# Weight-block sums by accumulating DMAs, and two plain pairs ahead of the first seven-product chunk

## The chip, the core and the metric

One NeuronCore of a Trainium2 chip. The metric is the device time of one execution in microseconds, the median of the runs. The engines are named PE (matmuls), VectorE (DVE), ScalarE (ACT), GpSimd (POOL) and SyncE (SP).

## The reference, cut to what matters

Four transformer-like layers over 640 tokens (512 of a sample, 128 of a prompt) with 1024 features, in float32. Layer kinds are conv, pool, attention, conv; each layer ends in a gated feed-forward stage:

```python
hs = modulate(rms_norm(xs, norm2_w[i]), mod_s[3], mod_s[4])
xs = xs + mod_s[5] * swiglu(hs, ffn_in_w[i], ffn_out_w[i])   # the same for xp
# swiglu: hidden = silu(h @ gate_w) * (h @ up_w);  out = hidden @ out_w
# ffn_in_w: (1024, 2 * 2816), ffn_out_w: (2816, 1024)
```

The 2816 hidden features are 22 tiles of 128. A tile needs one tile of gate columns and one of up columns: a pair. The change touches the feed-forward input product of the last layer only.

## The kernel before

**Precision and the plain way.** Each float32 product is made of three float32r matmuls: high part by high part, high by low, low by high. ScalarE makes the high part of weights (a copy into w_hi), VectorE the low part (raw minus w_hi, into w_lo). In the plain way, of layers 0 to 2, weights go in units of 128 columns by 1024 rows, four to a quad, two pairs to a quad. `h_unit` runs 8 x 3 x 2 = 48 matmuls a unit (L700, 320 columns, and L701), so 96 a pair.

**Seven products.** In the last layer (`FIRST_SEVEN = [3, 3, 3, 0]`) all 22 pairs, in chunks of 8, 8 and 6, are made by a seven-product scheme of Strassen's kind (Winograd's form). Tokens are cut into two halves of 320 (and two columns for the shift), features into two halves of 512, gate and up are the two column halves. `product` (L754) runs 4 x 3 = 12 matmuls of 322 columns, and a pair has 7 products, 84 matmuls. For this the kernel needs sums of activations, t1 to t4 (four rows each), and sums of weight blocks, s1 to s4:

- s1 = up rows 0-511 + up rows 512-1023, in `tmp[:, 2]` (product 5; for the very first pair tmp[:, 3])
- s3 = gate first half - up first half, in place of up's first half (product 7)
- s2 = s1 - gate first half, in place of gate's first half (product 6)
- s4 = gate second half - s2, in place of gate's second half (product 3)

Products 1, 2 and 4 use blocks as loaded. GpSimd makes the sums with four 128 x 512 instructions a pair, in `s13` and `s24`: L592 (s1), L596 (s3), L603 (s2), L607 (s4). Each waits on `block_lo_ready` for the split of the block that it overwrites.

**Order.** `ORDER` gives the blocks: for p >= 1, (p,1), (p-1,4), (p,5), (p,6), (p,2), (p,7), (p,3). w_hi and w_lo hold four blocks; block b goes where block b-4 was, once that product is done. ScalarE (`block_hi`, L1252) and VectorE (`block_lo`, L1817) work strictly in their written order between the copy-outs: on ScalarE after (p,7) comes the split of (p+1,5), after (p,3) that of (p+1,6), then the copy-out of product (p+1,1) (L1299) and the split of (p+1,2). The split of (p,3) stands ahead of the copy-outs L1306 and L1310, on the second of which PE's product (p,7) waits. SyncE reloads the raw slots of a pair (two 512 KB loads) when block (p,4) is split. L1923 on VectorE adds product 7 to the up half; PE's product (p,4) waits for it.

**The start of the stage.** GpSimd makes t1 to t4 out of h as its rows become ready (L554 to L569), VectorE the last row (L1861 to L1866); ScalarE and VectorE split them (`turn_step`: t1 after the first unit of the last output quad, a row of t2 to t4 after each other, the last in the seven-product chunk). PE begins the stage with product (0,1) while rows of h still come.

Of the kernel before, what the change touches and what calls it, by code (L numbers as in the profile page):

```python
# [26 lines left out]
KD = D // P  # L27
# [81 lines left out]
SEVEN = 7  # L109
T_STEPS = 4 * HALF  # L110
# [26 lines left out]
ORDER = {n: _order(n) for n in (CHUNK, LAST)}  # L137
# [4 lines left out]
LAYER_S = [sum(max(FT - CHUNK * FIRST_SEVEN[n], 0) for n in range(i)) for i in range(DEPTH + 1)]  # L142
# [3 lines left out]
def _pairs_before(layer, c):  # L146
    return LAYER_S[layer] + CHUNK * (c - FIRST_SEVEN[layer])
# [19 lines left out]
def build(nc, d):  # L167
    with ExitStack() as ctx:
# [99 lines left out]
        s_made = sem("s_made")  # L268
# [118 lines left out]
        def s1_home(p, norm):  # L387

            return tmp[:, 3 if norm and p == 0 else 2, 0:HW]

        def block_source(p, m, norm):

            j = 2 * (p % 2)
            return {1: raw[:, j, 0:HW], 6: raw[:, j, 0:HW], 2: raw[:, j, HW:2 * HW], 3: raw[:, j, HW:2 * HW],
                    7: raw[:, j + 1, 0:HW], 4: raw[:, j + 1, HW:2 * HW], 5: s1_home(p, norm)}[m]
# [11 lines left out]
        def bank_y(p, norm):  # L407

            return ps[:, 2, 0:TW] if norm and p == 0 else ps_sum[:, 1, 0:TW]
# [119 lines left out]
        def _(pool):  # L529
# [45 lines left out]
            def s13(layer, c, p, q, n, norm):  # L575

                first, j, qq = _pairs_before(layer, c), 2 * (p % 2), q + p // 2
                gate_w, up_w = raw[:, j, :], raw[:, j + 1, :]
                pool.wait_ge(raw_in[j], 16 * qq + 16)
                pool.wait_ge(raw_in[j + 1], 16 * qq + 16)  # L580
                if norm and p == 0:
                    if KIND[layer] == "attn":
                        pool.wait_ge(head_ready, HEAD_ROWS)
                elif norm and p == 1:
# [24 lines left out]
            def begin_chunk(layer, c, q, n, norm, turns):  # L609

                s13(layer, c, 0, q, n, norm)
                if turns:
                    t234_of(layer, 2)
                s24(layer, c, 0, n, norm)

            def rest_of_chunk(layer, c, q, n, norm, triples):

                for p in range(1, n):
                    if p % 2 == 1 and p > 1 and p // 2 < len(triples):
                        ada_triple(triples[p // 2])  # L620
                    s13(layer, c, p, q, n, norm)
                    s24(layer, c, p, n, norm)
# [8 lines left out]
            for layer in range(DEPTH):  # L631
# [34 lines left out]
                for c in range(FIRST_SEVEN[layer], 3):  # L666
                    tiles, norm = CHUNK if c < 2 else LAST, c == 0
                    qc = q + c * (Q_IN + Q_OUT)
# [13 lines left out]
        def _(pe):  # L682
# [30 lines left out]
            def h_quads(q, n, count, first=True, late=False):  # L713
# [21 lines left out]
                with pe.Fori(1 if first else 0, count) as i:  # L735
                    for j in range(4):
                        h_unit(i + q, j, n)

            def seven_chunk(layer, c, q, n, norm):

                first, place = _pairs_before(layer, c), PLACE[n]
                row, turns = 2 * layer + 1, c == FIRST_SEVEN[layer]

                def product(p, m, out, a_hi, a_lo, begin, row_ready=None):
# [4 lines left out]
                    for k in range(HALF):  # L749
                        if row_ready is not None:  # L750
                            pe.wait_ge(h_ready, row_ready + k + 1)
# [10 lines left out]
                def p1(p):  # L762
# [5 lines left out]
                    if norm and p == 1:  # L768
                        pe.wait_ge(c11_out, first + 1)
                    product(p, 1, bank_x(p), h_hi[:, 0:HALF, 0:TW], h_lo[:, 0:HALF, 0:TW], True, H_BASE[row] if turns and p == 0 else None)  # L770

                def p2(p):

                    if norm and p == 0:
                        pe.wait_ge(freed[1], 2 * q + 1)
                    else:
                        pe.wait_ge(c11_out, first + p)
                    if norm and p == 1:
                        pe.wait_ge(rms_ready, row + 1)
                    product(p, 2, bank_y(p, norm), h_hi[:, HALF:KD, 0:TW], h_lo[:, HALF:KD, 0:TW], True,  # L780
                            H_BASE[row] + HALF if turns and p == 0 else None)
# [21 lines left out]
                def p6(p):  # L803

                    pe.wait_ge(p1_kept, first + p + 1)
                    if p == 0:
                        turned_rows(T_STEPS - 2)
                    product(p, 6, bank_x(p), t2_hi, t2_lo, False)

                def p7(p):  # L810

                    pe.wait_ge(u2_kept, first + p + 1)
                    if p == 0:
                        turned_rows(T_STEPS - 1)
# [5 lines left out]
                if norm:  # L820
                    sum_features(sq_sum, sq_added, (KD - 1) * (row + 1), sum_ready)
# [347 lines left out]
            for layer in range(DEPTH):  # L1169
# [34 lines left out]
        def _(act):  # L1204
# [23 lines left out]
            def ffn_in_quad(q, i, products, tiles=(KD,) * 4, norm=None):  # L1228
                for j in range(4):
                    step(q, j, tiles[j])  # L1230
                    if j == 0 and norm:
# [11 lines left out]
            def block_hi(n, b, first, q, norm):  # L1243
# [6 lines left out]
                else:  # L1250
                    act.wait_ge(s_made, 4 * (first + p) + {5: 1, 7: 2, 6: 3, 3: 4}[m])
                act.activation(block_home(w_hi, n, b), block_source(p, m, norm), ACT.Copy).then_inc(block_hi_ready, 1)  # L1252

            def first_blocks(layer, c, q, j):

                n = CHUNK if c < 2 else LAST
                for b in {2: (0, 1), 3: (2, 3)}[j]:
                    block_hi(n, b, _pairs_before(layer, c), q, c == 0)
# [1358 lines left out]
```

## Time and profile before

| what | value |
|---|---|
| time, median of 3 runs | 2658.68 us (2658.28 to 2659.0) |
| span of the profiled execution | 2656.5 us, instructions 45073 |
| what lies around its span, to the median | 2.2 us |
| granted TensorE clock, mean | 0.994 |
| seven-product stage, first to last L754 | 2194.8 to 2601.6 us |

The profiled execution is one execution; its span goes from the first to the last instruction. A line such as L754 is a line of the kernel. Matmuls overlap, so a busy PE still has a cadence that is to be read from counts.

### The profile page before, as it was taken

How to read it: one execution, taken by the hardware profiler on the slowest of the kernel's cores; microseconds unless marked ns; L12 is line 12 of the kernel's file. 1: busy time of each engine (PE TensorE's matmuls, PEld its weight loads, DVE VectorE, ACT ScalarE, POOL GpSimd, SP SyncE). 2: the span in 40 equal slices, each digit the busy share in tenths (PEclk: the TensorE clock that was granted, in tenths of full speed). 3: DMA queues.
4: the chain of work that ended last, by engine and by line, in shares of the span. 5: the costliest groups of instructions: out<-in, count | busy, mean ns of one | idle time of the engine just before them, and what ended most of it. 6: DMA issues, size and time to landing. Idle time of an engine off the chain costs nothing.

```text
span 2656.5 us, 45073 instructions
## 1 busy us (share of the span) xinstructions
PE 2626.7 (99%) x17374; PEld 2554.8 (96%) x17374; DVE 1869.1 (70%) x3118; ACT 895.5 (34%) x1346; POOL 252.5 (10%) x300
## 2 busy tenths in 40 slices
PE   9999999999999999999999999999999998999998
PEld 5999999999999999999967999999999997999998
DVE  5898778676586776846775678777465559949486
ACT  4223331212342222124675431221232235425253
POOL 0000001000000000000000000000000034324040
PEclk9999999999999999999999999999999998999999
DMA  7444445354224544422102245444222221212222
GB/s 301 150 144 141 127 134 174 126 159 140 75 80 127 158 150 127 151 69 84 40 13 80 89 136 163 135 139 138 59 88 75 71 64 48 97 63 81 95 75 77
DMA packets 85625, 295.19 MB, mean 111 GB/s; under 512 B 10112, under 2 KB 13312, under 8 KB 85248
## 3 DMA queue, kind: packets, MB, share of 16 engines
q1 hardware_dynamic: 60016, 200.74, 23.0%
q0 software_dynamic: 25488, 92.81, 11.2%
q8 instruction: 79, 1.29, 0.2%
q14 instruction: 42, 0.34, 0.0%
HBM read 290.63 MB, written 2.88 MB: 110 GB/s over the span
## 4 chain that ended last, share of the span: by engine, by line
PE 89%; DVE 6%; issue 2%; ACT 1%; POOL 1%; DMA 1%; DVEq 0%; ACTq 0%; SPq 0%; POOLq 0%
PE ps L700 39%; PE ps L701 39%; PE ps L754 4%; DVE w_lo L1817 1%; PE ps_x L1010 1%; PE ps L986 1%; PE ps_sum L754 1%; DVE tmp L1935 1%; PE ps_sum L997 1%; PE ps L1142 1%; DMA mix<-in_ada_head 1%; DVE w_lo L1702 0%; PE ps L1093 0%; ACT w_hi L1207 0%; PE ps L867 0%
## 5 line engine op out<-in xcount | busy, mean ns | idle before, releaser
L1702 DVE TENSOR_TENSOR w_lo<-raw,w_hi 128x1024 fp32r<-128x1024 f32 (+2 forms) x315 | 376.1, 1194 | 459.2 <-ACT w_hi L1207 458.0
L1207 ACT ACTIVATE w_hi<-raw 128x1024 fp32r<-128x1024 f32 (+2 forms) x315 | 325.1, 1032 | 910.9 <-PE ps L701 899.1
L700 PE MATMUL ps<-h_hi,w_hi 128*128 128x320 f32 x1536 | 479.9, 312 | 0.7 <-DVE h_lo L2031 0.7
L701 PE MATMUL ps<-h_lo,w_hi 128*128 128x322 f32 x1536 | 478.5, 312 | 0.0
L700 PE MATMUL ps<-h_lo,w_hi 128*128 128x320 f32 x1536 | 477.4, 311 | 0.0
L701 PE MATMUL ps<-h_hi,w_lo 128*128 128x322 f32 x1536 | 477.4, 311 | 0.0
L700 PE MATMUL ps<-h_hi,w_lo 128*128 128x320 f32 x1536 | 477.1, 311 | 0.0
L701 PE MATMUL ps<-h_hi,w_hi 128*128 128x322 f32 x1536 | 476.1, 310 | 0.0
L1730 DVE CUSTOM_DVE_ANT_0 ps_x<-ada_w,cond 128x1024 f32<-128x1024 f32 x354 | 436.0, 1232 | 33.5 <-DVE tmp L1778 12.9
L701 PEld LDWEIGHTS ps<-h_hi,w_hi 128*128 128x128 f32 x1536 | 291.1, 190 | 0.5
L701 PEld LDWEIGHTS ps<-h_hi,w_lo 128*128 128x128 f32 x1536 | 291.3, 190 | 0.0
L700 PEld LDWEIGHTS ps<-h_hi,w_hi 128*128 128x128 f32 x1536 | 289.6, 189 | 1.3 <-DVE h_lo L2031 0.8
L700 PEld LDWEIGHTS ps<-h_hi,w_lo 128*128 128x128 f32 x1536 | 290.5, 189 | 0.0
L701 PEld LDWEIGHTS ps<-h_lo,w_hi 128*128 128x128 f32 x1536 | 289.6, 189 | 0.0
L700 PEld LDWEIGHTS ps<-h_lo,w_hi 128*128 128x128 f32 x1536 | 288.4, 188 | 0.0
L700 PE MATMUL ps<-g_hi,w_hi 128*128 128x320 f32 x884 | 274.7, 311 | 3.1 <-DVE x L1991 2.6
L701 PE MATMUL ps<-g_hi,w_lo 128*128 128x320 f32 x884 | 273.6, 309 | 0.0
L700 PE MATMUL ps<-g_hi,w_lo 128*128 128x320 f32 x884 | 273.5, 309 | 0.0
L701 PE MATMUL ps<-g_lo,w_hi 128*128 128x320 f32 x884 | 273.4, 309 | 0.0
L701 PE MATMUL ps<-g_hi,w_hi 128*128 128x320 f32 x884 | 273.4, 309 | 0.0
L700 PE MATMUL ps<-g_lo,w_hi 128*128 128x320 f32 x884 | 273.4, 309 | 0.0
L540 POOL DMA_DIRECT2D ada_w<-in_ada_w x177 | 94.0, 531 | 1729.7 <-DVE ada_raw L1730 1351.7
(244 smaller groups left out, 4220.1 us busy)
## 6 DMA issues: line engine op xcount, KB each, us to landing
raw<-in_weights SPq DMA_DIRECT2D x323, 512.0 KB, 3.6
ada_w<-in_ada_w POOLq DMA_DIRECT2D x177, 512.0 KB, 3.8
raw<-in_weights SPq DMA_DIRECT2D x32, 384.0 KB, 3.0
mix<-in_ada_head SPq DMA_DIRECT2D x16, 512.0 KB, 10.4
x<-in_x SPq DMA_DIRECT2D x8, 320.0 KB, 9.8
out_y<-mix SPq DMA_DIRECT2D x16, 160.0 KB, 1.9
mix<-in_spread SPq DMA_DIRECT2D x1, 1088.0 KB, 5.6
cond<-in_cond SPq DMA_DIRECT2D x1, 1024.0 KB, 14.9
```

What stands on the lines that cost most here:

```text
L540: pool.dma_start(ada_w[:, j * D:(j + 1) * D], d["ada_w"][ADA_N * qa + (j - LEAD)]).then_inc(ada_in[j], 16)
L700: pe.matmul(ps[:, 2 * slot, 0:TA], w[:, slot, ws], a(k)[:, 0:TA], start=begin, stop=end)
L701: mm = pe.matmul(ps[:, 2 * slot + 1, 0:width - TA], w[:, slot, ws], a(k)[:, TA:width], start=begin, stop=end)
L754: mm = pe.matmul(out, w[:, ws], a[:, k, :], start=begin and k == 0 and i == 0, stop=k == HALF - 1 and i == 2, skip_group_check=True)
L986: pe.matmul(out[:, 0:TS], row[:, qt * P:(qt + 1) * P], key[:, 0:TS], start=True, stop=True)
L997: mm = pe.transpose(sum_flat[:, k * P:(k + 1) * P], tmp[:, n % 2, k * P:(k + 1) * P], ident[:])
L1010: pe.matmul(ps_rot, val, of_sample[:, k, :], start=(k == 0), stop=(k == 4))
L1142: mm = pe.matmul(head_row[g % 2], cond_k[:, 2 * pair + k, :], head_w[:, n % HEAD_SLOTS, k * HEAD_W * P:(k + 1) * HEAD_W * P], start=(pair ...
L1207: act.activation(w_hi[:, j % 2, 0:tiles * P], raw[:, j, 0:tiles * P] if src is None else src, ACT.Copy).then_inc(w_hi_ready, 1)
L1702: dve.tensor_tensor(w_lo[:, j % 2, 0:tiles * P], raw[:, j, 0:tiles * P] if src is None else src, w_hi[:, j % 2, 0:tiles * P].bitcast(F32), ...
L1730: dve.tensor_tensor_reduce(ada_products, ada_w[:, j * D:(j + 1) * D], cond[:, v, :], 1.0, 0.0, ALU.mult, ALU.add, ada_raw[:, j, v:v + 1]). ...
L1817: dve.tensor_tensor(block_home(w_lo, n, b), block_source(p, m, norm), block_home(w_hi, n, b).bitcast(F32), ALU.subtract).then_inc(block_lo ...
```

## The change

Constants and chunk sizes: the first chunk of the last layer gets two plain pairs (one quad) ahead of 6 seven-product pairs; the chunks are then 6, 8 and 6.

The sums are made by DMAs issued from GpSimd's queue, 256 KB each. An accumulating DMA adds its source to its destination. s1 is a copy of up's first half from the weights in HBM into tmp[:, 2] and an addition of up's second half from HBM; s3 adds gate's first half from HBM to the raw up half; s2 adds s1 (SBUF) to gate's first half; s4 adds the new s2 (SBUF) to gate's second half. All are sums, with no difference: s3 = gate + up, s2 = gate + s1, s4 = second half + s2. The signs go into the activations: t1, t2 and t4 are split with a factor of -1, and the up result takes a factor of -1 when it is scaled by rinv. (The host hands in the up columns as before.) GpSimd waits for the copy of s1 before it issues the addition to it, for s1 before s2, and for s2 before s4.

```diff
+T1_ROWS = [(), (0,), (1, 2), (3,)]
+T2_ROWS = [(), (0, 1), (2,), (3,)]
+PLAIN_PAIRS = 2
+SEVENS = [CHUNK - PLAIN_PAIRS, CHUNK, LAST]
...
+            def s13(layer, c, p, q, n):
                 first, j, qq = _pairs_before(layer, c), 2 * (p % 2), q + p // 2
+                gate_w, up_w = d["weights"][4 * qq + j], d["weights"][4 * qq + j + 1]
+                if p == 0 and c == 0:
                     pool.wait_ge(sum_ready, 2 * layer + 2)
                 elif p:
                     pool.wait_ge(block_lo_ready, SEVEN * first + PLACE[n][p - 1, 5] + 1)
+                    pool.wait_ge(s2_made, 16 * (first + p))
                 elif c > FIRST_SEVEN[layer]:
                     pool.wait_ge(block_lo_ready, SEVEN * first)
-                pool.tensor_tensor(s1_home(p, norm), up_w[:, 0:HW], up_w[:, HW:2 * HW], ALU.add).then_inc(s_made, 1)
+                    pool.wait_ge(s2_made, 16 * first)
+                pool.dma_start(s1_home, up_w[:, 0:HW]).then_inc(s1_begun, 16)
+                pool.wait_ge(raw_in[j + 1], 16 * qq + 16)
+                pool.dma_start(raw[:, j + 1, 0:HW], gate_w[:, 0:HW], accum_op=ALU.add).then_inc(s3_made, 16)
+                pool.wait_ge(s1_begun, 16 * (first + p + 1))
+                pool.dma_start(s1_home, up_w[:, HW:2 * HW], accum_op=ALU.add).then_inc(s1_made, 16)
+            def s2(layer, c, p, n):
                 first, j = _pairs_before(layer, c), 2 * (p % 2)
                 pool.wait_ge(block_lo_ready, SEVEN * first + PLACE[n][p, 1] + 1)
-                pool.wait_ge(s_made, 4 * (first + p) + 1)
-                pool.tensor_tensor(up_w[:, 0:HW], gate_w[:, 0:HW], up_w[:, 0:HW], ALU.subtract).then_inc(s_made, 1)
+                pool.wait_ge(s1_made, 16 * (first + p + 1))
+                pool.dma_start(raw[:, j, 0:HW], s1_home, accum_op=ALU.add).then_inc(s2_made, 16)
+            def s4(layer, c, p, n):
                 pool.wait_ge(block_lo_ready, SEVEN * first + PLACE[n][p, 2] + 1)
-                pool.wait_ge(s_made, 4 * (first + p) + 3)
-                pool.tensor_tensor(gate_w[:, HW:2 * HW], gate_w[:, HW:2 * HW], gate_w[:, 0:HW], ALU.subtract).then_inc(s_made, 1)
+                pool.wait_ge(s2_made, 16 * (first + p + 1))
+                pool.dma_start(raw[:, j, HW:2 * HW], raw[:, j, 0:HW], accum_op=ALU.add).then_inc(s4_made, 16)
...
-                        seven_chunk(layer, c, q, tiles, c == 0)
+                        h_quads(q, 2 * layer + 1, PLAIN_PAIRS // 2, late=kind == "pool")
+                        seven_chunk(layer, c, q + PLAIN_PAIRS // 2, tiles - PLAIN_PAIRS)
...
-                act.activation(t1_hi[:, k, :], t2_full[:, k, :], ACT.Copy).then_inc(t_hi_ready, 1)
+                act.activation(t1_hi[:, k, :], t2_full[:, k, :], ACT.Identity, scale=-1.0).then_inc(t_hi_ready, 1)
...
+                if turns:
+                    act.wait_ge(unit_done, 4 * q)
+                    for k in range(HALF):
+                        t3_hi_of(layer, k)
                 after_p1(0)
                 after_p5(0)
                 only_refill(0, 2)
+                if turns:
+                    for k in range(HALF):
+                        t4_hi_of(layer, k)
...
-                    dve.tensor_tensor(up_row(p)[:, 0:TA], bank_x(p)[:, 0:TA], rinv[:, 0:TA], ALU.mult).then_inc(c21_out, 1)
+                    dve.scalar_tensor_tensor(out=up_row(p)[:, 0:TA], in0=bank_x(p)[:, 0:TA], scalar=-1.0, in1=rinv[:, 0:TA],
+                                             op0=ALU.mult, op1=ALU.mult).then_inc(c21_out, 1)
```

The second part of the diff is PE's order for the first chunk, the third ScalarE's, the last VectorE's. GpSimd's order for pair 0 is s13, t2 to t4 of row 2, s2, the same of row 3, s4; for every later pair s13, s2, s4. The turned rows are split in other places: t1 in the last output quad (`T1_ROWS`: rows after its second, third and fourth unit), t2 in the plain quad (`T2_ROWS`), t3 and t4 in the chunk, t3 once the plain quad's last unit is done. GpSimd makes the last row too, where VectorE did. Gone too are the waits of the first chunk on rows of h and on the sum of squares (`norm`, `row_ready`), since the plain quad stands there now.

## Rows read from the trace of the kernel before

**Rows 1.** The page, busy us of each engine and their share of the span.

```profile
PE 2626.7 (99%) x17374; PEld 2554.8 (96%) x17374; DVE 1869.1 (70%) x3118; ACT 895.5 (34%) x1346; POOL 252.5 (10%) x300
```

**Rows 2.** By stretch: PE, PEld, DVE, ACT, POOL busy (count), PEclk, DMA share, GB/s.

```profile
2176.00:2230.00 54.00, 37.93 (x193) 36.17 (x192) 41.78 (x59) 23.36 (x45) 30.90 (x26) 0.78 0.09 29
2230.00:2242.00 12.00, 12.00 (x83) 12.00 (x82) 11.70 (x18) 6.25 (x13) 4.52 (x4) 1.00 0.25 88
262.00:304.00 42.00, 42.00 (x282) 41.68 (x281) 34.28 (x52) 16.44 (x21) 2.27 (x5) 1.00 0.41 126
1476.00:1530.00 54.00, 54.00 (x364) 53.68 (x363) 38.20 (x58) 23.43 (x29) 1.59 (x3) 1.00 0.32 98
```

**Rows 3.** PE of line L754 alone, by stretch; seven-product chunks 1 and 2.

```profile
2350.00:2480.00 130.00, 100.53 (x672) 1.00 0.23 82
2500.00:2620.00 120.00, 75.15 (x504) 1.00 0.23 75
```

**Rows 4.** Waits of PE, 2155 to 2232 us: total, times, longest.

```profile
PE ps L754 <- issue: 5.5, 1, 5.5
PE ps L754 <- ACT tmp L1299: 4.0, 1, 4.0
PE ps L754 <- DVE x L1991: 3.8, 1, 3.8
PE ps L700 <- DVE x L1991: 2.6, 1, 2.6
```

**Rows 5.** The timeline of GpSimd, one pair of chunk 1.

```profile
2410.17 1.29 POOL L607 TENSOR_TENSOR raw<-raw 128x512 f32<-128x512 f32 x1 [4.75 <-DVE w_lo L1817]
...
2415.25 1.29 POOL L596 TENSOR_TENSOR raw<-raw 128x512 f32<-128x512 f32 x1 [2.10 <-DVE w_lo L1817]
2416.62 1.61 POOL L603 TENSOR_TENSOR raw<-tmp,raw 128x512 f32<-128x512 f32 x1
2422.99 1.29 POOL L607 TENSOR_TENSOR raw<-raw 128x512 f32<-128x512 f32 x1 [4.75 <-DVE w_lo L1817]
```

**Rows 6.** Who waited for VectorE line L1923, whole span: us, times.

```profile
  PEld ps L754: 2.1, 5
```

**Rows 7.** The timeline of ScalarE, the same pair.

```profile
2418.32 0.63 ACT L1252 ACTIVATE w_hi<-raw 128x512 fp32r<-128x512 f32 x1 [1.28 <-POOL raw L603]
2420.04 0.44 ACT L1299 ACTIVATE tmp<-ps 128x320 f32<-128x320 f32 x1 [1.08 <-PE ps L754]
2420.37 0.63 ACT L1252 ACTIVATE w_hi<-raw 128x512 fp32r<-128x512 f32 x1
```

**Rows 8.** The timeline of VectorE, the same pair.

```profile
2419.76 0.68 DVE L1817 TENSOR_TENSOR w_lo<-tmp,w_hi 128x512 fp32r<-128x512 f32 x1
```

**Rows 9.** VectorE groups in a plain stage of layer 2, 1500 to 1600 us.

```profile
L1778 DVE TENSOR_TENSOR tmp<-ps,tmp 128x640 f32<-128x640 f32 x15 | 12.2, 815 | 0.0
...
L1789 DVE SCALAR_TENSOR_TENSOR tmp<-tmp,bias 128x512 f32<-128x512 f32 x7 | 5.3, 752 | 0.9
...
L1789 DVE SCALAR_TENSOR_TENSOR tmp<-tmp,bias 128x128 f32<-128x128 f32 x7 | 2.4, 346 | 0.0
```

**Rows 10.** ScalarE groups, 1500 to 1600 us.

```profile
L1219 ACT ACTIVATE g_hi<-tmp 128x640 f32 x7 | 5.2, 741 | 24.1 <-DVE tmp L1789 24.1
```

**Rows 11.** VectorE line L1941: durations in ns, minimum, median, maximum.

```profile
L1941 DVE TENSOR_TENSOR g_lo<-tmp,g_hi x22: 810/1894/1909, 2234.4 to 2604.7; 128x640 fp32r<-128x640 f32 x22
```

**Rows 12.** The DMA view, issues: count, KB each, median us to landing.

```profile
raw<-in_weights SPq DMA_DIRECT2D x323, 512.0 KB, 3.6
ada_w<-in_ada_w POOLq DMA_DIRECT2D x177, 512.0 KB, 3.8
...
mix<-in_spread SPq DMA_DIRECT2D x1, 1088.0 KB, 5.6
...
raw<-in_weights SPq DMA_DIRECT2D x4, 256.0 KB, 2.5
```

**Rows 13.** GpSimd line L540, issues of 512 KB: ns, minimum, median, maximum.

```profile
L540 POOL DMA_DIRECT2D ada_w<-in_ada_w x177: 530/530/699, 36.0 to 1824.3; - x177
```

More of the change, by code:

```diff
@@ L405, in bank_z @@
             return ps[:, 2 * (p % 2) + 1, 0:TW]
-        def bank_y(p, norm):
-            return ps[:, 2, 0:TW] if norm and p == 0 else ps_sum[:, 1, 0:TW]
+        bank_y = ps_sum[:, 1, 0:TW]
         def gate_row(p):
@@ L734, in h_quads, with seven_chunk, product @@
                         h_unit(q, j, n, first=True)
[L735 to L739, printed above, removed]
+                if count > 1 or not first:
+                    with pe.Fori(1 if first else 0, count) as i:
+                        for j in range(4):
+                            h_unit(i + q, j, n)
+            def seven_chunk(layer, c, q, n):
                 first, place = _pairs_before(layer, c), PLACE[n]
-                row, turns = 2 * layer + 1, c == FIRST_SEVEN[layer]
-                def product(p, m, out, a_hi, a_lo, begin, row_ready=None):
+                turns = c == FIRST_SEVEN[layer]
+                def product(p, m, out, a_hi, a_lo, begin):
                     b = place[p, m]
@@ L767, in p1 @@
                         pe.wait_ge(c21_out, first + p - 1)
-                    if norm and p == 1:
-                        pe.wait_ge(c11_out, first + 1)
-                    product(p, 1, bank_x(p), h_hi[:, 0:HALF, 0:TW], h_lo[:, 0:HALF, 0:TW], True, H_BASE[row] if turns and p == 0 else None)
+                    product(p, 1, bank_x(p), h_hi[:, 0:HALF, 0:TW], h_lo[:, 0:HALF, 0:TW], True)
                 def p2(p):
[L774 to L781, printed above, removed]
+                    pe.wait_ge(c11_out, first + p)
+                    product(p, 2, bank_y, h_hi[:, HALF:KD, 0:TW], h_lo[:, HALF:KD, 0:TW], True)
                 def p3(p):
@@ L1226, in gate, with ffn_in_quad @@
                 a.then_inc(gate_ready, 1)
-            def ffn_in_quad(q, i, products, tiles=(KD,) * 4, norm=None):
+            def ffn_in_quad(q, i, products, tiles=(KD,) * 4, norm=None, first=None, turns=None):
                 for j in range(4):
                     step(q, j, tiles[j])
+                    if first is not None and j >= 2:
+                        first_blocks(*first, j)
                     if j == 0 and norm:
@@ L1241, in ffn_in_quad, with block_hi @@
                         g_hi_of(pair_b[:, j // 2, :], bass.ds(2 * i + j // 2, 1) if not isinstance(i, int) else slice(2 * i + j // 2, 2 * i + j // 2 + 1))
-            def block_hi(n, b, first, q, norm):
+                    if turns is not None:
+                        for k in T2_ROWS[j]:
+                            t2_hi_of(turns, k)
+            def block_hi(n, b, first, q):
                 p, m = ORDER[n][b]
@@ L1271, in t234_hi_of @@
-                act.activation(t4_hi[:, k, :], t4_full[:, k, :], ACT.Copy).then_inc(t_hi_ready, 1)
-            def turn_step(layer, j):
-                if j == 0:
-                    for k in range(HALF):
-                        t1_hi_of(layer, k)
-                else:
-                    t234_hi_of(layer, j - 1)
-            def seven_chunk(layer, c, q, n, r, g, tiles, norm):
-                first, place, row = _pairs_before(layer, c), PLACE[n], 2 * layer + 1
+                act.wait_ge(t_lo_ready, T_STEPS * LAYER_T[layer] + 2 * HALF + k + 1)
@@ L1290, in refill @@
                     for b in REFILL[n][place[p, m]]:
-                        block_hi(n, b, first, q, norm)
+                        block_hi(n, b, first, q)
                 def after_p1(p):
-                    if norm and p < 2:
-                        act.wait_ge(sq_added, (KD - 1) * (row + 1))
-                    else:
-                        act.wait_ge(product_ready, r + p - 1)
+                    act.wait_ge(product_ready, r + p - 1)
                     done(p, 1)
@@ L1791, in times, with ffn_in_quad @@
                 v.then_inc(product_ready, 1)
-            def ffn_in_quad(q, i, count, pairs, products, ada=None, tiles=(KD,) * 4, norm=None):
+            def ffn_in_quad(q, i, count, pairs, products, ada=None, tiles=(KD,) * 4, norm=None, first=None, turns=None):
                 for j in range(4):
+                    if first is not None and j >= 2:
+                        first_blocks(*first, j)
                     step(q, j, tiles[j])
@@ L1948, in seven_chunk @@
                 after_p2(0)
-                if norm:
-                    inverse_rms(row)
+                if turns:
+                    for k in range(HALF):
+                        t4_lo_of(layer, k)
                 after_p6(0)
@@ L2321, in attention @@
                         shift_lo(2 * layer + 1)
-                    out_quad(q + half, 4 * half, 2 * layer + 1, gate_of(GATE1), (KD, KD, 0, 0) if half and seven else (KD,) * 4, True,
-                             first=(layer, 0, q + Q_OUT) if half and seven else None, turns=layer if half and seven else None)
+                    out_quad(q + half, 4 * half, 2 * layer + 1, gate_of(GATE1), (KD,) * 4, True, turns=layer if half and seven else None)
             def tail(q, gate):
```

197 lines of the change are left out of this document (94 added, 103 removed).

## The prediction

> **What bounds the kernel now.** I read the page's busy shares first: PE 99%, VectorE 70%, GpSimd 10% [rows 1]. A core in which PE never rests gains only where matmuls disappear, where PE waits, or where its clock is low. So I looked for stretches in which PE does fewer matmuls than its cadence allows. The view by stretches shows one around the change: from 2176 to 2230 us PE ran 193 matmuls in 54 us at a mean granted clock of 0.78 [rows 2]. At the cadence of the seven-product pairs, 672 matmuls in 100.5 us or 0.150 us each [rows 3], these are worth 29 us: 25 us are lost. The waits of PE say how: four waits of 2.6, 3.8, 5.5 and 4.0 us, 15.9 in all [rows 4]; the rest is half clock (0.78 is 44% of the stretch at 1.2 GHz, its other level being 2.4). The same passage into a plain feed-forward stage, in layers 0 and 2, has PE busy throughout at clock 1.00 [rows 2]. That is the loss the two plain pairs can take away.
>
> Then the seven-product stage. A pair is seven products of 12 matmuls: 100.53/8 = 12.57 us, 1.80 us a product. GpSimd's rows show a period of 12.82 us (2410.17 to 2422.99) [rows 5]: PE is the bound, with short waits for L1923 on VectorE, 2.1 us in five times over the whole stage [rows 6].
>
> **What the change takes away and adds, term by term.**
>
> Two plain pairs: 2 x 96 matmuls at 0.148 us (364 in 54 us [rows 2]) = 28.5 us, against 2 x 12.57 = 25.1: **+3.4**.
>
> The passage: PE now works on the plain quad while t1 and t2 are made. What stays is the end of the quad. After its last unit ScalarE splits two blocks (0.63 us each [rows 7]), VectorE makes their low parts (0.68 each [rows 8]), takes the row out (0.82) and multiplies (0.75 + 0.35) [rows 9], about 4.1 us after that unit with the small steps between; ScalarE then makes g_hi, 0.74 [rows 10], five turned rows and the copy that the product (0,6) waits for, six of about 0.44 [rows 7]: 7.5 us, where PE wants (0,6) after three products, 5.4. A gap of 2.1, one of about 1 at (0,7), 2 more for the half clock that such a gap brings (24 us at half clock beside 15.9 of waits in [rows 2, 4]), 1 in the output quad, where t1 on VectorE is now spread over three units: 6 of the 25 stay. **-19**.
>
> GpSimd's arithmetic: while it reads SBUF, VectorE's 640-column subtraction takes 1.89 us instead of 0.81 (median and minimum of L1941 [rows 11]). The Trainium skill has the rule (SBUF — State Buffer, the part on who interferes with whom: a VectorE instruction with two SBUF inputs contends with a GpSimd instruction that reads SBUF); the trace agrees. VectorE isn't the bound, so it is worth at most the waits for L1923: **-2.1 if nothing else holds the pairs, 0 if something does**. The extra multiplications by -1 lie on VectorE operations that exist already: 0.
>
> The DMAs decide. Each pair now needs five of 256 KB on GpSimd's queue, in code order: s1 copy, s3 add, s1 add, s2 add, s4 add. The old four instructions took 1.3 to 1.7 us each, and GpSimd had 7 us of idle time a pair (4.75 before L607, 2.10 before L596) [rows 5].
>
> - A plain 256 KB load took 2.5 us from SyncE's queue; GpSimd's 512 KB took 3.8 where SyncE's took 3.6 [rows 12]. So the copy: 2.7 us, 0.53 of it issue [rows 13]. From 512 to 1088 KB the time grew by 2.0 us, 0.87 for 256 KB [rows 12].
> - No row shows an accumulating DMA or one that reads SBUF to write SBUF. Below, it costs what a copy does, 2.7. Its destination must be read besides the source, a second 256 KB: 2.7 + 0.87 = 3.6. If the write also comes in turn: 4.4. I take L = 3.6, the size with an extra stream, and keep 2.7 and 4.4 for the range. The Trainium skill (DMA: Bandwidth & Descriptors, anatomy of one DMA) gives 2.0 us + bytes/436 GB/s, an estimate of 2.6 us here, with no other term for an addition; by that the first rival below would hold, at 2641.
>
> Now the loop. Let t0 be the end of the low part of block (p,2); before, the s4 instruction starts there (2410.17, 2422.99) [rows 5]. GpSimd issues s4(p), then the s1 copy of pair p+1, which sits behind it in the queue although it needs only block (p,5) and s2(p). The copy lands at 0.6 + 2.7 + 1.17 = t0+4.5; 1.17 is s4's data, 2 x 0.87, less the 0.6 of head start. s3 lies beside it. The s1 add lands at t0+8.1, the s2 add at t0+11.7. Then ScalarE must split (p+1,6), copy out the first product and split (p+1,2), and VectorE makes the low part: 0.63 + 0.33 + 0.63 + 0.68 and small steps = 2.4 [rows 7, 8]. Period: 14.05 us. Before, L603 ended at t0+8.07 and the next t0 was at 12.82, so 4.75 us were there where 2.4 suffice: slack of 2.3 us, and the DMAs eat 3.6. To this come SyncE's two weight loads a pair, 512 KB each, on the same 16 engines: I add 1.0 (bounds 0 and 1.7, the data time of an addition doubled). **Period 15.05 us, 2.5 more than PE needs.**
>
> How often? Pair 0 of each of the three chunks (6, 8 and 6 pairs) has its sums made during the quad before. Pair 1 is 0.9 us within its time: s2(1) lands at 1.3 + 12.65 = 13.95 after the chunk's start, and (1,6) can wait for it until 9 x 1.8 - 1.4 = 14.8. Pair 2 stalls 1.6, each later one 2.5: 9.1 + 14.1 + 9.1 = **+32.3**. These stalls fall on PE before products (p,6) and (p,7), the latter because ScalarE holds at block (p,3) for s4 (3.6 after t0) with the copy-outs for (p,7) behind it.
>
> Sum: +32.3 + 3.4 - 19 = +16.7 us. On the profiled execution, 2656.5 us, that is 2673; on the median of the runs, which lies 2.2 above, **2675**.
>
> **The rivals.**
>
> *The accumulating DMAs are hidden* (ends on the other side). If an addition costs a copy's 2.7 us, s2 lands at 0.6 + 2.7 + 0.3 + 5.4 = t0+9.0, the period of the loop is 11.4, or 12.4 with 1.0 of loads, and PE stays the bound. Then -19 + 3.4 - 2.1 = -17.7: 2641. For it: GpSimd idle more than half of each pair [rows 5]; DMA share in this stretch only a quarter [rows 2]. Against: the chain is three landings deep, and share says nothing of latency. It decides at 14 x g - 2.7 = 15.6, so a surplus g of 1.3 us a pair, which is L = 3.2 us; my two-stream size is above that, a copy's below.
>
> *Additions much slower than two streams.* L = 4.4, with s3 0.7 in the way of the s1 add and 1.7 of loads: s2 lands at t0+14.8, period 18.9, +85 - 15.6 = +70: 2729. Each further us of L adds 3 us a pair, 42 in all, so L = 5.1 gives 2760. For it: the kind of DMA isn't in the trace at all.
>
> *Half clock on top.* The gaps of 2.6 to 5.5 us brought about 6 us of half clock each [rows 2, 4]. If every stall of 2.5 does this, PE needs 12.6 + 3 = 15.6 a pair instead of 15.05: +8 more, 2683. It would add to the forecast, not change its sign; counted in its range.
>
> *The change doesn't do what it says* (additions in order but the plain quad stalls like the old start): the passage gives back only 10 of 19; with the main loop 2684. Against: layers 0 and 2.
>
> **Numbers.** Tell-apart bound: 0.2%, 5.3 us. Forecast (additions between 3.3 and 4 us) 0.38, giving 2664 to 2695; much slower 0.20; hidden 0.30; between hidden and forecast, near break-even, 0.12, of which 0.08 is within 0.2% and 0.04 below. So faster 0.34, same 0.08, slower 0.58. Range 2638 to 2755: it takes in the hidden case and L up to 5.
>
> **What would show it.** In the new trace: in the 54 us around the passage some 330 matmuls or more instead of 193, at a clock near 1; five GpSimd DMA issues a pair with additions landing at 3.6 us; a period of some 15 us between s4 issues; ScalarE's split waiting for DMA rather than for GpSimd; PE waits for w_lo of (p,6). VectorE's L1941 row falls to 0.81. I am wrong if additions land in under 3.2 us, or if the queue doesn't delay the copy behind s4.

## The result and the profile after

The changed kernel takes 2725.62 us (median of 4 runs, 2720.09 to 2725.99); the kernel before took 2658.53 in the same session (4 runs, 2658.28 to 2659.0). The ratio is 1.0247, interval 1.0233 to 1.0262: 67 us slower. The profiled execution took 2725.99, its span 2724.3. Direction and range were right, the size was not: +67 against a forecast of +17.

The page of the kernel after, busy time of each engine, beside [rows 1]:

```profile
PE 2650.6 (97%) x17398; PEld 2572.0 (94%) x17398; DVE 1800.8 (66%) x3097; ACT 882.3 (32%) x1330; POOL 211.0 (8%) x317
```

PE has the 24 more matmuls that two plain pairs cost, and rests 74 us instead of 30. VectorE and GpSimd are both less busy, and yet the kernel is slower: the busy shares don't show the cause.

By stretch, after (columns as in [rows 2]), and then the third stretch in the kernel before. In the kernel after, the second chunk's pairs run from 2370.8 to 2509.4 us, so the third stretch has 20 us of the output product at its end; the fourth is one long period of those pairs:

```profile
2176.00:2230.00 54.00, 52.56 (x352) 51.86 (x351) 43.34 (x65) 26.27 (x49) 32.32 (x32) 1.00 0.39 91
2230.00:2242.00 12.00, 10.96 (x72) 10.43 (x72) 7.65 (x15) 5.96 (x12) 3.17 (x4) 1.00 0.75 180
2390.00:2530.00 140.00, 120.03 (x704) 116.80 (x704) 72.95 (x134) 48.31 (x93) 25.62 (x32) 0.89 0.55 128
2408.90:2429.30 20.40, 16.95 (x89) 16.48 (x89) 9.52 (x18) 6.57 (x14) 4.10 (x6) 0.80 0.52 117
```

```profile
2390.00:2530.00 140.00, 139.72 (x944) 139.15 (x943) 101.12 (x153) 53.86 (x94) 39.20 (x27) 1.00 0.24 83
```

The first line is the passage from the output product into the stage: 352 matmuls where [rows 2] has 193. The plain quad nearly fills it, as in layers 0 and 2. The third line is the loss: in 140 us PE ran 704 matmuls instead of 944, at a granted clock of 0.89. What PE waited for there (waits of PE, 2190 to 2680 us, in us, times, longest), and what ScalarE waited for:

```profile
PE ps L765 <- DVE w_lo L1829: 38.9, 16, 3.6
PE ps L765 <- ACT tmp L1311: 20.1, 15, 2.6
PE ps L765 <- ACT tmp L1300: 1.4, 1, 1.4
```

```profile
ACT w_hi L1261 <- DMA raw<-tmp: 73.2, 15, 6.5
...
ACT w_hi L1261 <- DMA raw<-raw: 58.7, 19, 3.7
ACT w_hi L1261 <- DMA tmp<-in_weights: 43.4, 15, 7.6
```

PE's 38.9 us for w_lo (nearly all ahead of product (p,6)) and 20.1 us for the copy-out L1311 (ahead of product (p,7)) are the two places that the prediction named. One step back, ScalarE stands before its split for each of the three sums in turn: s2 (`raw<-tmp`) 73.2 us, s4 (`raw<-raw`) 58.7, s1 (`tmp<-in_weights`) 43.4. Nothing waits for s3.

GpSimd's timeline over one pair shows the loop itself. L615 is s4, L595 the s1 copy, L598 s3, L601 the s1 addition, L608 s2; each row is an issue (for a DMA the second number is the time of the issue), and the bracket the idle time before it:

```profile
2464.63 0.85 POOL L615 DMA_DIRECT2D raw<-raw  x1 [7.66 <-DVE w_lo L1829]
2465.17 0.89 POOL L595 DMA_DIRECT2D tmp<-in_weights  x1
2465.72 1.23 POOL L598 DMA_DIRECT2D raw<-in_weights  x1
2469.75 0.86 POOL L601 DMA_DIRECT2D tmp<-in_weights  x1 [2.80 <-DMA tmp<-in_weights]
2474.14 0.86 POOL L608 DMA_DIRECT2D raw<-tmp  x1 [3.54 <-DMA tmp<-in_weights]
2481.87 0.85 POOL L615 DMA_DIRECT2D raw<-raw  x1 [6.87 <-DVE w_lo L1829]
```

From one s4 to the next 17.24 us. Over all 17 such intervals inside the chunks, the means from the starts of the issues are 5.45 from s4 to the s1 addition, 4.56 on to s2 and 7.79 on to the next s4: a period of 17.81 (16.0 to 20.3). PE needs 12.57 for a pair: 5.24 too many, 17 times, is 89 us. The DMA view gives the landings, all issued by GpSimd:

```profile
tmp<-in_weights POOLq DMA_DIRECT2D x40, 256.0 KB, 4.3
...
raw<-in_weights POOLq DMA_DIRECT2D x20, 256.0 KB, 5.1
raw<-tmp POOLq DMA_DIRECT2D x20, 256.0 KB, 5.2
raw<-raw POOLq DMA_DIRECT2D x20, 256.0 KB, 3.3
```

The first row mixes the s1 copy (median 4.4) with the s1 addition (3.8, by source line). s4 lands in 3.3. s2 is mostly issued just after SyncE's weight loads of 512 KB (in the pair above 2.2 us after two of them) and has a median of 5.2. In the four cases in which the last load was over 6 us old it landed in 3.2 to 3.3; with a load at most 2.6 us old it took 4.9 to 6.8, but for one of 3.8.

VectorE's subtraction, which took 1894 ns in the median [rows 11], is relieved as forecast, and nothing comes of it:

```profile
L1935 DVE TENSOR_TENSOR g_lo<-tmp,g_hi x20: 815/819/826, 2240.4 to 2672.3; 128x640 fp32r<-128x640 f32 x20
```

### The profile page after: what moved, and what is told of

It reads as the page before. It is cut to its first block and busy times, and to the rows that moved or that the text cites. A ratio compares the mean times of both kernels' runs of the same rounds, so it can differ in the third digit from the quotient of the medians.

```text
span 2724.3 us, 45071 instructions
## 1 busy us (share of the span) xinstructions
PE 2650.6 (97%) x17398; PEld 2572.0 (94%) x17398; DVE 1800.8 (66%) x3097; ACT 882.3 (32%) x1330; POOL 211.0 (8%) x317
## 3 DMA queue, kind: packets, MB, share of 16 engines
q8 instruction: 79, 1.29, 0.2%
## 5 line engine op out<-in xcount | busy, mean ns | idle before, releaser
L712 PE MATMUL ps<-h_hi,w_hi 128*128 128x320 f32 x1568 | 490.0, 313 | 0.7 <-DVE h_lo L2027 0.7
L713 PE MATMUL ps<-h_lo,w_hi 128*128 128x322 f32 x1568 | 488.5, 312 | 0.0
L712 PE MATMUL ps<-h_lo,w_hi 128*128 128x320 f32 x1568 | 487.3, 311 | 0.0
L713 PE MATMUL ps<-h_hi,w_lo 128*128 128x322 f32 x1568 | 487.3, 311 | 0.0
L712 PE MATMUL ps<-h_hi,w_lo 128*128 128x320 f32 x1568 | 487.0, 311 | 0.0
L713 PE MATMUL ps<-h_hi,w_hi 128*128 128x322 f32 x1568 | 486.0, 310 | 0.0
L713 PEld LDWEIGHTS ps<-h_hi,w_hi 128*128 128x128 f32 x1568 | 297.2, 190 | 0.6
L713 PEld LDWEIGHTS ps<-h_hi,w_lo 128*128 128x128 f32 x1568 | 297.3, 190 | 0.0
L712 PEld LDWEIGHTS ps<-h_hi,w_hi 128*128 128x128 f32 x1568 | 295.6, 189 | 1.4 <-DVE h_lo L2027 0.8
L712 PEld LDWEIGHTS ps<-h_hi,w_lo 128*128 128x128 f32 x1568 | 296.5, 189 | 0.0
L713 PEld LDWEIGHTS ps<-h_lo,w_hi 128*128 128x128 f32 x1568 | 295.6, 189 | 0.0
L712 PEld LDWEIGHTS ps<-h_lo,w_hi 128*128 128x128 f32 x1568 | 294.4, 188 | 0.0
```

The costliest lines, as they stand in the source:

```text
L712: pe.matmul(ps[:, 2 * slot, 0:TA], w[:, slot, ws], a(k)[:, 0:TA], start=begin, stop=end)
L713: mm = pe.matmul(ps[:, 2 * slot + 1, 0:width - TA], w[:, slot, ws], a(k)[:, TA:width], start=begin, stop=end)
```

## The experiments

Each kernel is the kernel after with the edit shown. Ratios are against the kernel before, run on the same chip.

**1. The sums by GpSimd's arithmetic.** Plain pairs, signs and orders stay; the DMAs go. s3 and s4 are changed in the same way, on the blocks already loaded, and s3 waits again for the split of block (p,1), as in the kernel before.

```diff
-pool.dma_start(s1_home, up_w[:, 0:HW]).then_inc(s1_begun, 16)
-pool.dma_start(s1_home, up_w[:, HW:2 * HW], accum_op=ALU.add).then_inc(s1_made, 16)
+pool.tensor_tensor(s1_home, up_w[:, 0:HW], up_w[:, HW:2 * HW], ALU.add).then_inc(s1_made, 16)
...
-pool.dma_start(raw[:, j, 0:HW], s1_home, accum_op=ALU.add).then_inc(s2_made, 16)
+pool.tensor_tensor(raw[:, j, 0:HW], s1_home, raw[:, j, 0:HW], ALU.add).then_inc(s2_made, 16)
```

> The changed kernel with its two plain pairs, signs and turned rows, but the four sums made by GpSimd's additions again. Theory (the loss is the chain of DMA landings, the passage itself gains): the pairs return to 12.6 to 12.8 us, the passage keeps its 352 matmuls in 54 us, 2658.5 - 22 + 3.4 = about 2640 us. Rival (the plain quad, the signs or the new order of the turned rows cost too): 2655 us or more, with PE waits at the start of the first chunk.

Measured: 2646.36 us (5 runs, 2646.27 to 2646.62), ratio 0.9954 (0.994 to 0.9967). So the change is two changes of opposite sign: the plain pairs with their orders give 12 us, the DMAs cost 79. It is 6 us above the 2640 that I expected. The 140 us in and behind the second chunk are whole again, but the passage isn't as good as with DMAs:

```profile
2176.00:2230.00 54.00, 48.21 (x315) 47.31 (x314) 42.50 (x54) 24.39 (x45) 32.55 (x28) 0.96 0.15 49
2390.00:2530.00 140.00, 139.26 (x939) 138.40 (x939) 97.89 (x150) 53.25 (x93) 37.83 (x27) 1.00 0.26 83
```

```profile
2198.69 1.29 POOL L595 TENSOR_TENSOR tmp<-raw 128x512 f32<-128x512 f32 x1 [5.23 <-DMA raw<-in_weights]
2210.87 1.62 POOL L599 TENSOR_TENSOR raw<-raw 128x512 f32<-128x512 f32 x1 [10.89 <-DVE w_lo L1826]
2212.45 0.89 POOL L570 TENSOR_TENSOR mix<-h_hi,h_lo 128x322 f32<-128x322 f32 x1
```

GpSimd's timeline points at the cause. s3 of the first pair (L599) waits 10.89 us for the split of block (0,1), which not s3 but s2 behind it overwrites; the sums of turned rows 2 and 3 (from L570) stand behind it in GpSimd's order though they need nothing of it. With DMAs that wait falls on s2, which comes after row 2. Kernel 9 tests this.

**2. The order of the issues alone.** All sums stay DMAs. The s1 copy of the next pair goes ahead of s4, and s3 behind the s1 addition.

```diff
 for p in range(1, n):
...
-    s13(layer, c, p, q, n)
+    s1_copy(layer, c, p, q, n)
+    s4(layer, c, p - 1, n)
+    s1_add(layer, c, p, q, n)
+    s3(layer, c, p, q, n)
     s2(layer, c, p, n)
-    s4(layer, c, p, n)
+s4(layer, c, n - 1, n)
```

(`s13` was copy, s3, addition.)

> The changed kernel with the DMAs in another order on GpSimd's queue: the copy of s1 for pair p+1 is issued ahead of the s4 addition of pair p, and s3 behind the s1 addition. Theory (three landings in a row behind the split of block (p,2)): the copy starts some 2.4 us earlier and no longer waits behind s4's data; s2 to s2 is then 2.8 + 0.5 + 4.0 + 0.5 + 5.2 = 13.0 to 13.5 us instead of 17.2 to 18, the time 2650 to 2675 us. Rival (GpSimd's issue time or the 16 DMA engines are the limit, whatever the order): the same five DMAs a pair, so over 2710 us.

Measured: 2654.73 us (10 runs, 2652.17 to 2657.85), ratio 0.9986 (0.9977 to 0.9995): 71 us faster than the kernel after with the same DMAs. Over the 17 intervals the period falls from 17.81 to 13.62 us in the mean (12.45 to 16.78); below is a short one, 12.45 from copy to copy (L594 the copy, L623 s4, L599 the s1 addition, L604 s3, L616 s2). PE's waits fall from 61 to 12 us, 8.1 of them for the copy-out behind s4:

```profile
2409.36 0.57 POOL L594 DMA_DIRECT2D tmp<-in_weights  x1 [4.84 <-DMA raw<-tmp]
2411.38 0.86 POOL L623 DMA_DIRECT2D raw<-raw  x1 [1.45 <-DVE w_lo L1837]
2412.68 0.86 POOL L599 DMA_DIRECT2D tmp<-in_weights  x1 [0.43 <-DMA tmp<-in_weights]
2413.21 1.21 POOL L604 DMA_DIRECT2D raw<-in_weights  x1
2417.57 0.85 POOL L616 DMA_DIRECT2D raw<-tmp  x1 [3.14 <-DVE w_lo L1837]
2421.81 0.57 POOL L594 DMA_DIRECT2D tmp<-in_weights  x1 [3.40 <-DMA raw<-tmp]
```

```profile
PE ps L773 <- ACT tmp L1319: 8.1, 13, 1.9
```

The copy flies while GpSimd waits for block (p,2): when s4 is out, 0.43 us are left of it. In the kernel after, that whole landing lay behind s4. So 71 of the 87 us that lie between the kernel after and the best one below (kernel 10) come from where the landings stand in a queue that issues in order. The other 16 are the 1 us by which the mean period is still above PE's.

**3. The same transfers, adding nothing.** Every accumulating DMA becomes a plain copy of the same bytes.

```diff
-pool.dma_start(s1_home, up_w[:, HW:2 * HW], accum_op=ALU.add).then_inc(s1_made, 16)
+pool.dma_start(s1_home, up_w[:, HW:2 * HW]).then_inc(s1_made, 16)
```

and so for s2, s3 and s4.

> The changed kernel with every accumulating DMA replaced by a plain copy of the same bytes between the same places (the sums are missing, so the output is not the reference's). It measures what the adding itself costs. Theory of the prediction (the second stream costs 0.6 to 0.9 us a landing): s4's copy lands in 2.6 us instead of 3.3, the two additions in the chain gain as much, the period falls by about 2 us, time about 2698 us. Rival (the landing's fixed part and GpSimd's issue are all that counts): landings as before within 0.2 us, time over 2715 us.

Measured: 2670.87 us (4 runs, 2668.21 to 2675.83), ratio 1.0053 (1.0038 to 1.0067). The landings (rows as above):

```profile
tmp<-in_weights POOLq DMA_DIRECT2D x40, 256.0 KB, 3.1
raw<-in_weights POOLq DMA_DIRECT2D x20, 256.0 KB, 3.4
raw<-tmp POOLq DMA_DIRECT2D x20, 256.0 KB, 3.9
raw<-raw POOLq DMA_DIRECT2D x20, 256.0 KB, 2.3
```

By source line: s4 takes 2.3 against 3.3 us, so adding costs about 1.0 us, and an issue takes 0.54 instead of 0.86. The three landings of the loop are the s1 copy (3.3 against 4.4; it now follows an s4 that only copies), the s1 addition (2.9 against 3.8) and s2 (3.9 against 5.2): 3.3 us a pair, 17 times, is 56, and this kernel is 55 us faster than the kernel after (mean period 14.71). I had expected half of that, 2698 us: the copies land 0.9 to 1.3 us sooner, not 0.7. What is left, 24 us over kernel 1, is the chain in this order even at a copy's price.

**4. Without most of the weight loads.** In the chunks of seven-product pairs SyncE loads 64 KB a block instead of 512.

```diff
-                with sp.Fori(0, 2 * (Q_IN + Q_OUT)) as i:
-                    load(i + q, KD)
+                        with sp.Fori(1 if c == 0 else 0, Q_IN) as i:
+                            load(i + (q + c * (Q_IN + Q_OUT)), 1)
```

> The changed kernel, where SyncE's weight loads of the seven-product pairs fetch 128 columns instead of 1024 (64 KB instead of 512 KB; the rest of the weights is stale, so the output is not the reference's). Theory of contention with the loads: the s2 addition lands in 3.3 to 3.6 us instead of 5.2, the s1 addition a little earlier, period 17.5 to about 15.5, time about 2697 us. Rival (the landings are slow of themselves, or GpSimd's issue is): s2 stays near 5.2 us, time over 2715 us.

Measured: 2704.38 us (4 runs, 2700.07 to 2706.84), ratio 1.0166 (1.0151 to 1.0182): the loads cost 21 us, 1.25 in each of the 17 intervals. s2, the addition that they had beside them, now lands like s4 (the rows below). I had expected a period of 15.5 and 2697 us, and the mean period is 16.67: s2's landing is 1.8 us shorter in the mean, but those of the s1 copy and the s1 addition are 0.3 and 0.4 longer (4.85 and 4.38 against 4.56 and 3.95), for a reason that no run shows.

```profile
raw<-tmp POOLq DMA_DIRECT2D x20, 256.0 KB, 3.3
raw<-raw POOLq DMA_DIRECT2D x20, 256.0 KB, 3.3
```

**5. Two homes for s1, both s1 DMAs ahead of s4.** With two homes the s1 of the next pair needs not wait for this pair's s2.

```diff
+        def s1_home(pair):
+            return ada_w[:, pair % 2 * HW:pair % 2 * HW + HW]
...
 for p in range(1, n):
-    s13(layer, c, p, q, n)
     s2(layer, c, p, n)
+    if p + 1 < n:
+        s1_copy(layer, c, p + 1, q, n)
+        s1_add(layer, c, p + 1, q, n)
     s4(layer, c, p, n)
+    if p + 1 < n:
+        s3(layer, c, p + 1, q, n)
```

> The changed kernel with two homes for s1 (the modulation weights' tile, free in the last layer), so that s1 of pair p+1 is made beside pair p, and only s2 and s4 stay in the chain. Theory (chain of landings): the pairs are bound by PE at 12.6 us, 2640 to 2648 us, like the arithmetic or a little better since VectorE is not slowed. Rival (capacity of the DMA engines or of GpSimd's queue with 5 DMAs and 2 loads a pair): additions land later, period over 14 us, 2680 us or more.

Measured: 2693.24 us (4 runs, 2689.97 to 2693.83), ratio 1.0126 (1.0111 to 1.0142). A miss: I expected the best of the DMA versions and got one 38 us worse than kernel 2. GpSimd's timeline (L618 s2, L596 the copy, L601 the addition, L625 s4):

```profile
2406.82 0.86 POOL L618 DMA_DIRECT2D raw<-ada_w  x1 [6.22 <-DVE w_lo L1844]
2407.36 0.89 POOL L596 DMA_DIRECT2D ada_w<-in_weights  x1
2414.38 0.86 POOL L601 DMA_DIRECT2D ada_w<-in_weights  x1 [6.14 <-DMA ada_w<-in_weights]
2414.93 1.20 POOL L625 DMA_DIRECT2D raw<-raw  x1
```

The addition must wait for the landing of its own copy, 6.14 us, and s4, which is urgent, stands behind that wait. PE now waits for the copy-out behind s4, and hardly for w_lo (0.8 us):

```profile
PE ps L780 <- ACT tmp L1326: 33.3, 17, 4.3
```

The place behind s4 had been a bad one for the copy; the place ahead is just as bad for whatever contains a wait.

**6. The addition behind s4.** One DMA of kernel 5 moves (the edit is against kernel 5).

```diff
     if p + 1 < n:
         s1_copy(layer, c, p + 1, q, n)
-        s1_add(layer, c, p + 1, q, n)
     s4(layer, c, p, n)
     if p + 1 < n:
+        s1_add(layer, c, p + 1, q, n)
         s3(layer, c, p + 1, q, n)
```

> The version with two homes for s1, with one DMA moved: the s1 addition of pair p+1 stands behind the s4 addition of pair p instead of ahead of it, so that GpSimd no longer holds s4 back while it waits for the copy (6 us a pair in the two-home run before). Theory (head of the line blocking on GpSimd's in-order queue made the two-home version 2693 us): s4 goes out when block (p,2) is split, pairs at 12.6 to 13.2 us, 2643 to 2655 us. Rival (capacity of the 16 DMA engines): still over 2680 us.

Measured: 2654.79 us (12 runs, 2650.34 to 2665.53), ratio 0.9991 (0.9981 to 1.0). Moving one issue gives 38 us, which shows the reading of kernel 5. The second home gives nothing over kernel 2. PE's longest waits, in total, are again for that copy-out:

```profile
PE ps L780 <- ACT tmp L1326: 8.9, 12, 2.0
```

**7. ScalarE's order.** In kernel 6 PE waits for the copy-out ahead of (p,7), which stands behind the split of (p,3). So ScalarE does the copy-outs first (the edit is against kernel 6).

```diff
 def after_p5(p):
     done(p, 5)
-    refill(p, 5)
+    if p == 0:
+        refill(p, 5)
...
     act.activation(gate_row(p)[:, TA:TH], bank_x(p), ACT.Copy).then_inc(u2_kept, 1)
+    if p:
+        refill(p, 5)
     refill(p, 6)
```

> As the run before it, and ScalarE copies out products 5 and 6 of a pair before it waits for s4 to split block (p,3). Theory (the remaining PE waits are for the copy-out behind s4's landing, 8 us in the reordered run): those waits vanish, 3 to 8 us below the run before it. Rival (the time is set elsewhere): within 1 us of it.

Measured: 2660.73 us (11 runs, 2654.28 to 2663.88), ratio 1.0005 (0.9997 to 1.0014). I had expected 3 to 8 us less than kernel 6 and got 6 more. The wait for the copy-out is gone, and another has come:

```profile
PE ps L780 <- DVE w_lo L1847: 14.3, 17, 2.4
```

PE's timeline tells the 17 waits apart. Nine, of 0.3 to 0.8 us and 3.4 in all, stand before product (p,3) and are for the block of s4, whose own landing is that late. Eight, of 0.7 to 2.4 us and 10.9 in all, stand before product (p,6) and are for s2's block. GpSimd waited for the s1 addition's landing before it issued s2 in 11 pairs, 37.4 us, where kernel 6 has 1 pair and 2.9 us, and s2 landed in 4.8 us in the median against 3.7. So a wait behind one landing was taken away and the chain of the others took its place; why it is longer here than in kernel 6, with the same DMAs in the same order, was not tested.

**8. The same order of ScalarE on kernel 1.**

> GpSimd's additions with two plain pairs, with the same new order on ScalarE. PE waited there only 5.6 us at the start of the first chunk and 1.1 us at product 4. Theory: ScalarE is not late in the pairs, so within 1.5 us of 2646.4. Rival: ScalarE's order does matter there too, 2 us or more below.

Measured: 2647.01 us (5 runs, 2646.77 to 2647.08), ratio 0.9957 (0.9944 to 0.9969), kernel 1's time: where s4 takes 1.29 us on GpSimd, this order of ScalarE changes nothing.

**9. Kernel 1 with s3 of the first pair not held.** In the first pair of each chunk s3 goes out at once, and s2 takes over the wait.

```diff
-    pool.wait_ge(block_lo_ready, SEVEN * first + PLACE[n][p, 1] + 1)
+    if p:
+        pool.wait_ge(block_lo_ready, SEVEN * first + PLACE[n][p, 1] + 1)
     pool.wait_ge(s1_made, 16 * (first + p + 1))
```

> GpSimd's additions with two plain pairs; for pair 0 s3 no longer waits for the split of block (0,1) (10.9 us of idle GpSimd, with the turned rows 2 and 3 queued behind it); s2 waits for that split instead. Theory (the passage of the arithmetic version keeps a gap of 5.6 us before product (0,6), since t2 is late behind that wait): the gap shrinks to 2 us or less, 2641 to 2643 us. Rival (ScalarE's work after the plain quad sets the gap, as in the prediction's 2.1 us): 2645 us or more.

Measured: 2642.24 us (5 runs, 2642.11 to 2643.34), ratio 0.994 (0.9926 to 0.9953): 4.1 us better than kernel 1, as expected. PE's longest wait in the stage shrinks from 5.6 us (first row, kernel 1) to 3.3 (second, this kernel), where I had expected 2 or less:

```profile
PE ps L762 <- ACT tmp L1297: 5.6, 1, 5.6
```

```profile
PE ps L764 <- ACT tmp L1299: 3.3, 1, 3.3
```

So s3's wait was worth 2.3 us of that gap. In the rest, ScalarE's copy-out still stands behind g_hi and five turned rows, as the prediction had it.

**10. Each sum where it does best.** Kernel 2's order, with s1 and s3 by DMA and s2 and s4, the two that a split waits for within microseconds, by GpSimd.

```diff
+    pool.tensor_tensor(raw[:, j, 0:HW], s1_home, raw[:, j, 0:HW], ALU.add).then_inc(s2_made, 16)
...
+    pool.tensor_tensor(raw[:, j, HW:2 * HW], raw[:, j, HW:2 * HW], raw[:, j, 0:HW], ALU.add).then_inc(s4_made, 16)
```

> s1 and s3 by DMAs in the reordered way, s2 and s4 by GpSimd's additions. Theory (what is left of the loss in the reordered run is the landing of s4, 3.3 us against 1.3 us of GpSimd, and s2's landing): PE waits before product 7 vanish, passage at its short 1 to 2 us, VectorE less slowed than with four additions: 2640 to 2645 us. Rival (any DMA in the chain costs): 2650 us or more.

Measured: 2638.27 us (5 runs, 2637.85 to 2638.37), ratio 0.9923 (0.991 to 0.9937), 20 us faster than the kernel before and below the 2640 to 2645 that I expected: the best kernel here. The passage is as full as in the kernel after, and PE doesn't rest in the second stretch:

```profile
2176.00:2230.00 54.00, 52.44 (x351) 51.73 (x350) 43.97 (x64) 26.42 (x50) 36.30 (x32) 1.00 0.32 79
2390.00:2530.00 140.00, 140.00 (x948) 140.00 (x948) 86.67 (x150) 53.16 (x93) 34.51 (x34) 1.00 0.43 113
```

Over kernel 9 it gains 4.0 us, and by the lengths of the chunks 3.4 of them lie in the first one, where GpSimd also makes turned rows (77.67 us from its first to its last matmul against 81.03); in the other two together it is 0.9. Once the stage runs, then, s1 and s3 by DMA are hardly better than by arithmetic.

## Why the prediction was right in direction and wrong in size

**Where it failed: the term of the pairs' stalls, forecast at +32.3, measured at about +87.** The mechanism was right: the three landings in series, the copy stuck behind s4, PE waiting for w_lo and for the copy-out ahead of (p,7). That the order makes most of the loss is shown by kernel 2 (71 us with the same DMAs), that the landings make it is shown by kernels 1 and 3. The size, from measured pieces: from the first to the last matmul on turned rows the kernel after takes 451.4 us, kernel 10, with the same pairs and PE busy nearly throughout, 363.4; and the times differ by 87.4. The period was too short in every piece, and it counts 17 times:

| piece of the period | forecast | measured |
|---|---|---|
| s4 issue to s1 addition issue | 4.5 | 5.45 |
| s1 addition to s2 issue | 3.6 | 4.56 |
| s2 to the next s4 issue | 3.6 + 2.4 + 1.0 = 7.0 | 7.79 |
| period | 15.05 | 17.81 |
| intervals that stall | 14, the first of each chunk spared | 16, and one by 0.9 us |

The pieces, in means over the 17 intervals, landing by landing:

- *The s1 copy at 2.7 us plus s4's data* gave 3.9 from its own issue; it took 4.56: 0.7 more.
- *No time between a landing and the next issue* was wrong. GpSimd issued the addition 0.3 us after the copy's landing, and s2 0.6 us after the addition's: 0.9 a period where the forecast had 0.
- *L = 3.6, the addition as a copy with an extra stream,* was nearly right: 3.95 for the s1 addition, and a median of 3.3 for s4. As a difference to a copy I had 0.9, and kernel 3 shows 1.0.
- *The loads at 1.0* were about right as a sum (1.25 an interval, kernel 4). s2, on which they fall, took 5.27 against my 3.6 + 1.0: 0.7 more.
- *From s2's landing to the next s4* it took 2.5 (2.2 to 2.9) against 2.4.

Together 2.8 us: the period was 17.81 and not 15.05.

*The count* was wrong too. Pair 1 was to be within its time by 0.9 us in each chunk. By that model a period longer by 2.8 lets it stall 1.9, and the sum is 14 x 5.24 + 3 x 1.9 = 79. Measured against the same intervals of kernel 10 (mean 12.74), the 17 are longer by 86: 74 in the 14 that the forecast had stall, and 12 in the three first ones, 0.9, 5.2 and 6.2 us (18.05 and 19.08 between the s4 issues in the second and third chunk, against 12.88 and 12.87). So in these two chunks pair 1 had no slack at all; why was not tested. Of the 55 us that the term was short, then, 47 are the length of the period and 8 the slack.

**The passage, -19**, was -22 to -23. PE is idle 1.4 us in the first stretch (busy 52.56 of 54) and does 72 matmuls of 0.15 us in the next 12, 1.2 short, where I had left 6 in all. The gap before (0,6) came where I had it, behind ScalarE's turned rows, and was 1.4 us instead of 2.1; the one at (0,7) and the half clock didn't come (the granted clock is 1.00). With arithmetic the same gap is larger: 3.3 us in kernel 9, and 5.6 in kernel 1, where GpSimd is also held by s3.

**The plain pairs, +3.4,** fit, but were not measured by themselves: kernel 10 is 20.3 us faster than before, and 3.4 - 22.5 - 2.1 (the waits for L1923, which can return only once nothing else holds the pairs) is -21.2. That last term was forecast in just this form: -2.1 or 0. In the kernel after, where the landings hold the pairs, nothing of it is gained.

**The rivals.** *Hidden* (2641) doesn't happen with these DMAs in this order: it asked for additions under 3.2 us, the quickest median is 3.3, and even plain copies give 2671. The Trainium skill (DMA: Bandwidth & Descriptors, anatomy of one DMA) has 2.0 us + bytes/436 GB/s, by my estimate 2.6 us for 256 KB. The copy from SBUF to SBUF takes 2.3 in kernel 3 and the same with an addition 3.3, so the rule is near for a copy and has no term for what the addition adds. *Much slower than two streams* (2729) names nearly the time that came, but not its cause: it rested on L = 4.4 for every addition and 1.7 of loads; additions alone took 3.3 to 3.8, and its period of 18.9 is a microsecond too long. It also let pair 1 go free; by its own model that pair would have stalled 3 us in each chunk, 2741 in all. That its 2729 lies near the measured 2726 is luck. *Half clock on top*: it came in part. The clock is 0.89 over 140 us, and 0.80 over one long period of 20.4 us in which PE did 89 matmuls, but 1.00 over another of 18.2 us (2234.1 to 2252.3) with waits of 1.0 and 3.5. It costs little on top: the period is set by the landings, 17.8 is over the 15.6 that PE needs with half clock, and the one piece in which a product of PE stands, from s2's landing to the next s4, is 0.1 over the forecast. *The change doesn't do what it says* is out: 352 matmuls in the passage.

**What stays open.** Now and then a copy lands late: in the stage of the kernel after, one s1 addition was issued only 6.7 us after the s3 issue ahead of it, where 4.0 is usual, and s1 copies took up to 6.2 us. It happens in kernel 4 too, so not for the full weight loads; the cause was not found. Kernels in which PE hangs on DMA landings also spread (kernel 6 over 15 us, kernel 2 over 6), while those with GpSimd's arithmetic in the late sums (kernels 1, 8, 9 and 10) stay within 1.3.

## What to carry to other kernels

Replace an engine's instruction by a DMA only where its result is wanted well after a landing's time, and keep the instruction where something waits sooner: here an accumulating DMA of 256 KB took the engine 0.9 us to issue and 3 to 5 us until its data could be used, where the instruction took 1.3 for both. When DMAs depend on each other through one in-order issuing engine, draw the loop with every landing and every wait in it before anything else, put each issue that is ready ahead of the next wait, and nothing that waits ahead of something urgent; here the order alone was worth 71 us with the same transfers. When a wait has been taken away, look again at what PE waits for now, product by product (kernel 7). And multiply small errors by the number of turns: 2.8 us a turn, in pieces of a microsecond and less, was most of the difference between +17 and +67.

## What the runs showed of the hardware

- An accumulating DMA of 256 KB from SBUF to SBUF lands in 3.3 us where the copy takes 2.3, and its issue occupies GpSimd for 0.86 us instead of 0.54.
- Loads of 512 KB that SyncE has issued shortly before lengthen such a landing: s2 took 5.2 us in the median (up to 6.8), 3.2 to 3.3 in the same kernel where the last load was over 6 us old, and 3.3 with loads of 64 KB (kernel 4).
- GpSimd issued a dependent DMA 0.3 us after the landing of the s1 copy and 0.6 us after that of the s1 addition (means of 17, kernel after).
- With DMAs in place of GpSimd's four instructions, VectorE's 640-column subtraction takes 0.82 us in all 20 cases; with two of the four left (kernel 10) it is still 0.82 in the median, but up to 1.91.
- PE's mean granted clock over the whole run is 0.989 in the kernel after, where PE waits twice in most pairs (38.9 us in 16 waits and 20.1 in 15, the longest 3.6), 0.994 in kernel 4 (29.9 in 17 and 17.7 in 15, the longest 2.6) and 0.998 where the waits in the stage are 2.0 us at most (kernels 2, 6 and 10).
